# Moving three modulation chunks and one expert's gate load in a two-layer diffusion step on one core

## The reference, cut to what matters

```python
def ada_modulation(cond, w, b):
    m = jax.nn.silu(cond) @ w + b                 # 1024 -> 6 * 1024, for each layer and each of two conds
    ...
for l in range(DEPTH):                            # DEPTH = 2
    sh1, sc1, g1, sh2, sc2, g2 = ada_modulation(cond, ada_w[l], ada_b[l])
    h = modulate(x, norm_mix_g[l], sh1, sc1)
    m = attention(h) if l == 0 else multi_scale_pool(h)
    x = x + g1 * m
    h = modulate(x, norm_ffn_g[l], sh2, sc2)
    x = x + g2 * hierarchical_moe(h, ...)         # 4 groups x 8 experts, top 2 in the best group
```

## Time and profile before

| | us |
|---|---|
| three runs | 866.87, 872.73, 871.26 |
| median | 871.26 |
| profiled execution, its own time | 872.78 |
| its span | 870.7 |
| bytes moved by DMA in it | 294.42 MB |

### The profile page before, as it was taken

One profiled execution on the slowest core, in us unless ns is written; L12 is line 12 of the kernel. 1 busy time (PEld: TensorE's weight loads), 2 busy tenths in 40 slices (PEclk: granted clock), 3 DMA queues, 4 the chain that ended last, 5 costly groups with the idle time before them and its releaser, 6 DMA issues.

```text
span 870.7 us, 12882 instructions
## 1 busy us (share of the span) xinstructions
PE 731.4 (84%) x4560; PEld 405.2 (47%) x4560; DVE 352.0 (40%) x830; ACT 141.3 (16%) x342; POOL 175.7 (20%) x275
## 2 busy tenths in 40 slices
PE   4899989999976999999889763877899999797760
PEld 3333433467834655555445431735555545344430
DVE  2222548642245244444333332556244444333233
ACT  3111154531352000000000001544000000000000
POOL 0000400000002143333323120001133343332220
PEclk9999999999986899999999996787799999999995
DMA  9999849841864899999999953976699999999935
GB/s 345 428 435 422 234 151 415 315 194 47 362 269 164 323 418 419 419 416 420 417 418 422 420 238 130 419 325 205 214 421 416 421 415 423 419 422 419 414 131 217
DMA packets 41979, 294.42 MB, mean 338 GB/s; under 512 B 10872, under 2 KB 12336, under 8 KB 22864
## 3 DMA queue, kind: packets, MB, share of 16 engines
q1 hardware_dynamic: 29248, 275.51, 77.7%
q0 software_dynamic: 10880, 13.26, 5.0%
q10 hardware_dynamic: 1808, 5.06, 1.4%
HBM read 293.24 MB, written 22.02 MB: 362 GB/s over the span
## 4 chain that ended last, share of the span: by engine, by line
PE 64%; DMA 19%; SPq 6%; DVE 5%; issue 3%; ACT 1%; POOL 0%; POOLq 0%; DVEq 0%
PE bank L1578 21%; PE bank L1602 9%; DMA ring<-in_moe_w_in 8%; PE bank L1326 7%; PE bank L1251 4%; DMA ring<-in_moe_w_out 4%; PE bank L1425 3%; DMA ring<-in_ada_w 3%; PE bank L1556 3%; SPq L392 2%; DMA adaw<-results 2%; PE bank L1433 2%; PE bank L1468 2%; PE bank L1385 2%; DMA adaw<-in_ada_w 1%
## 5 line engine op out<-in xcount | busy, mean ns | idle before, releaser
L1578 PE MATMUL bank<-ring,qkv 128*64 128x256 f32 x1440 | 175.2, 397 | 23.2 <-issue 11.6
L1578 PEld LDWEIGHTS bank<-ring,qkv 128*64 128x64 f32 x1440 | 110.2, 143 | 74.5 <-issue 22.4
L547 POOL DMA_INDIRECT results<-adaw,scur x65 | 67.8, 1043 | 286.4 <-DVE adaw L1124 253.2
L1101 DVE COPY qkv<-bank 128x512 f32<-128x512 f32 x64 | 44.3, 692 | 194.5 <-PE bank L1556 174.3
L805 ACT ACTIVATE qkv<-bank 128x128 f32<-128x128 f32 x64 | 17.8, 278 | 445.7 <-PE bank L1578 411.1
L1602 PE MATMUL bank<-ring,qkv 128*64 128x512 f32 x360 | 87.1, 604 | 1.2 <-DVE qkv L1113 0.8
L537 POOL DMA_INDIRECT adaw<-rows,gcur x57 | 59.2, 1039 | 44.3 <-issue 28.0
L1326 PE MATMUL bank<-ring,hT 128*128 128x512 f32 x144 | 63.5, 596 | 1.3 <-DVE hT L879 1.3
L1113 DVE COPY qkv<-bank 128x128 f32<-128x128 f32 x64 | 18.7, 292 | 75.7 <-PE bank L1587 74.5
L1122 DVE SCALAR_TENSOR_TENSOR adaw<-qkv,wcur 128x512 f32<-128x512 f32 x64 | 48.1, 752 | 2.3
L1124 DVE SCALAR_TENSOR_TENSOR adaw<-bank,wcur,adaw 128x512 f32<-128x512 f32 x64 | 48.1, 751 | 2.3
(11 more groups left out here) (236 smaller groups left out, 839.7 us busy)
## 6 DMA issues: line engine op xcount, KB each, us to landing
ring<-in_moe_w_in SPq DMA_DIRECT2D x44, 2048.0 KB, 25.2
ring<-in_moe_w_out SPq DMA_DIRECT2D x45, 1024.0 KB, 33.3
adaw<-in_ada_w SPq DMA_DIRECT2D x16, 2048.0 KB, 11.2
adaw<-in_moe_w_in SPq DMA_DIRECT2D x10, 2048.0 KB
ring<-in_ada_w SPq DMA_DIRECT2D x8, 2048.0 KB, 12.1
xT<-in_moe_w_in SPq DMA_DIRECT2D x10, 1536.0 KB
hT<-in_moe_w_out SPq DMA_DIRECT2D x10, 1024.0 KB
ring<-in_attn_w_qkv SPq DMA_DIRECT2D x3, 2048.0 KB, 36.1
```

The lines of the kernel that those rows point to most:

```text
L547: pool.indirect_dma_start(res, bass.IndirectOffsetOnAxis(ap=scur[:, p, :], axis=0), yout[:, p], None, bounds_check=res_limit, oob_is_err=F ...
L1101: V.tensor_copy(xgT[:, p], bank[2][:, :]).then_inc(xgT_ready, 1)
L1578: last = T.matmul(bank[p][64 * a:64 * a + 64, 0:2 * P], xk[:, k % 4, k // 4], w[k // IN_X if b > RING else 0][:, k % IN_X if b > RING else ...
```

## The change

The diff does four things. (1) Chunks 21 to 23 are no longer loaded in the attention and the router stage of layer 0. Their places become the gate places of ring places 3, 0 and 1; SP issues them after the weights of the first extra tile, each after the last `gate_up` that reads its place. TensorE multiplies them after the extra tiles, before it signals `extras_over`; the copy, the spreading and the bias of this set follow there. (2) The vectors of the first 21 chunks are added on VectorE ahead of the router. (3) SP loads the fifth expert's gate weights (L381 before, L383 after) in the attention, where it has waited for chunk 19's product. (4) In both layers `rows_by_token(4)` and `(5)` come after the prefix sum on TensorE. GpSimd's clearing of `xg` waits for chunk 20 and no longer for 23.

```diff
@@ modulation chunks: places
-        ADA_AT = [TAIL, LEFT, RIGHT, HIGH0, HIGH1] + [(i + 2) % 3 for i in range(5, 2 * NCH - 2)] + [LEFT, LEFT]
+        TAIL, LEFT, RIGHT, HIGH0, HIGH1, RING3, RING0, RING1 = range(8)
+        ada_place += [ring[:, b, 0:KD * ACH] for b in (3, 0, 1)]
+        ADA_AT = [TAIL, LEFT, RIGHT, HIGH0, HIGH1] + [(i + 2) % 3 for i in range(5, 2 * NCH - 3)] + [RING3, RING0, RING1]
...
@@ SP
-            for i in range(8, 2 * NCH - 1):
+            for i in range(8, 2 * NCH - 3):
                 load_ada(i)
...
                 if l == 0:
+                    sp.wait_ge(ada_mm, 20)
                     load_out(l, 3, 3, s_wout[3])
                     sp.dma_start(ring[:, 3, KD * FE:2 * KD * FE], moe_w_in[l, 3, :, KD * FE:2 * KD * FE]).then_inc(s_win[3], 16)
+                    load_in(l, RING, RING, s_win[RING])
                     sp.wait_ge(pv_mm, NU // 4)
...
                     sp.wait_ge(ada_vec, 2)
-                    sp.wait_ge(ada_mm, 22)
...
-                load_in(l, RING, RING, s_win[RING])
-                if l == 0:
-                    load_ada(2 * NCH - 1)
...
-                    sp.wait_ge(ada_vec, 4)
+                    sp.wait_ge(ada_vec, 3)
...
                     load_extra(0)
+                if l == 0:
+                    for i, s in ((21, NE - 5), (22, NE - 2), (23, NE - 1)):
+                        sp.wait_ge(gu_mm, s + 1)
+                        load_ada(i)
@@ GpSimd
-                    pool.wait_ge(ada_mm, 24)
+                    pool.wait_ge(ada_mm, 21)
@@ ScalarE
-                if l == 0:
-                    set_copy(3)
                 for n in range(6):
                     keep(n)
...
                 extra_tiles(act, n_extra, extra)
+                if l == 0:
+                    set_copy(3)
@@ VectorE
-                if l == 0:
-                    dve.wait_ge(ada_vec, 4)
-                    modulation(2, 0, 5, 6)
-                    modulation(2, 1, 0, 6)
-                    V.memset(ss[:, 17:18], 0.0).then_inc(mods_ready, 1)
...
             norm_dve(0, 0, 4, 3, lambda k: hT[:, k, 0:CTX])
+            dve.wait_ge(ada_vec, 3)
+            modulation(2, 0, 5, 6)
+            vectors_of(2, 1, 0, 4 * KD + KD // 2)
+            V.memset(ss[:, 17:18], 0.0).then_inc(mods_ready, 1)
             router(0)
             experts(0)
...
             scales(1, 1, 8)
+            dve.wait_ge(ada_vec, 4)
+            vectors_of(3, 1, 4 * KD + KD // 2, 6 * KD)
             scales(1, 4, 24)
@@ TensorE
-                if l == 0:
-                    ada(21)
-                    ada(22)
...
-                rows_by_token(4)
-                rows_by_token(5)
-                if l == 0:
-                    ada(23)
-
                 pe.wait_ge(over_ready, l + 1)
...
                 last.then_inc(over_mm, 1)
+                rows_by_token(4)
+                rows_by_token(5)
...
-                if l == 0:
-                    vectors(3)
...
+                pe.wait_ge(mods_ready, 3 + l)
                 rows_T(0, 0, old=False)
...
                 extra_tiles(pe, n_extra, extra)
                 if l == 0:
+                    for i in range(SETS[3], 2 * NCH):
+                        ada(i)
                     T.matmul(bank[3][:, 0:2], ident, C("sel")[:, 0:2], start=True, stop=True).then_inc(extras_over, 1)
+                    vectors(3)
```

More of the change, by code:

```diff
@@ L198, in build @@
                      high[:, 0:KD * ACH], high[:, KD * ACH:KD * D]]
-        TAIL, LEFT, RIGHT, HIGH0, HIGH1 = range(5)
-        ADA_AT = [TAIL, LEFT, RIGHT, HIGH0, HIGH1] + [(i + 2) % 3 for i in range(5, 2 * NCH - 2)] + [LEFT, LEFT]
-        ADA_USE = [ADA_AT[:i + 1].count(ADA_AT[i]) for i in range(2 * NCH)]
+        TAIL, LEFT, RIGHT, HIGH0, HIGH1, RING3, RING0, RING1 = range(8)
+        ada_place += [ring[:, b, 0:KD * ACH] for b in (3, 0, 1)]
+        ADA_AT = [TAIL, LEFT, RIGHT, HIGH0, HIGH1] + [(i + 2) % 3 for i in range(5, 2 * NCH - 3)] + [RING3, RING0, RING1]
+        ADA_SIGNAL = [at if at < RING3 else at - RING3 for at in ADA_AT]
+        ADA_USE = [ADA_SIGNAL[:i + 1].count(ADA_SIGNAL[i]) for i in range(2 * NCH)]
         ADA_PRIOR = [max([j for j in range(i) if ADA_AT[j] == ADA_AT[i]], default=-1) for i in range(2 * NCH)]
@@ L238, in build @@
         SETS = (0, 4, 10, 21, 2 * NCH)
-        SET_BANK, VECTOR_BANK = (0, 1, 2, 0), (2, 0, 1, 1)
+        SET_BANK, VECTOR_BANK = (0, 1, 2, 0), (2, 0, 2, 2)
         def set_of(i):
@@ L373, in load_ada @@
                     sp.wait_ge(ada_mm, ADA_PRIOR[i] + 1)
-                sp.dma_start(ada_place[ADA_AT[i]], ada_w[i // NCH, i % NCH]).then_inc(s_adaw[ADA_AT[i]], 16)
+                sp.dma_start(ada_place[ADA_AT[i]], ada_w[i // NCH, i % NCH]).then_inc(s_adaw[ADA_SIGNAL[i]], 16)
             def load_in(l, e, b, arrived):
@@ L859, in modulation, with vectors_of @@
             def modulation(n, l, a, b):
-                cols = bank[VECTOR_BANK[n]][:, l * 2 * NMOD + 2 * a * KD:l * 2 * NMOD + 2 * b * KD]
-                m = mods[:, l, a * KD:b * KD, :]
+                vectors_of(n, l, a * KD, b * KD)
+            def vectors_of(n, l, a, b):
+                cols = bank[VECTOR_BANK[n]][:, l * 2 * NMOD + 2 * a:l * 2 * NMOD + 2 * b]
+                m = mods[:, l, a:b, :]
                 order(V.tensor_tensor(m, cols.rearrange("p (m c) -> p m c", c=2),
-                                      bias[:, l, a * KD:b * KD].unsqueeze(2).to_broadcast([P, (b - a) * KD, 2]), ALU.add))
+                                      bias[:, l, a:b].unsqueeze(2).to_broadcast([P, b - a, 2]), ALU.add))
             def scales(l, i, first):
@@ L1244, in ada @@
                     pe.wait_ge(cond_ready, 2)
-                pe.wait_ge(s_adaw[ADA_AT[i]], 16 * ADA_USE[i])
+                pe.wait_ge(s_adaw[ADA_SIGNAL[i]], 16 * ADA_USE[i])
                 out = bank[SET_BANK[n]]
@@ L1618, in _ @@
                 hidden_T(0, 0, old=False)
-                pe.wait_ge(mods_ready, 3 + l)
                 gate_rows()
```

## The result

| | before | changed |
|---|---|---|
| median of 20 runs each, us | 870.12 | 866.49 |
| lowest and highest | 866.87, 875.37 | 863.14, 871.51 |
| ratio, 95% interval | | 0.9949 [0.9931, 0.9967] |
| profiled execution, its own time | 872.78 | 863.50 |
| its span | 870.7 | 861.5 |

The change gains half a per cent, 2.9 to 6.0 us by the interval of the ratio (4.4 at its middle; the medians are 3.6 apart). The forecast of 864.3 has the sign, and the result lies in its range, but the gain in it was too large: 7.0, counted from the 871.26 of the three runs before, where twenty runs gave 870.12. From that base it would have been 863.1, 3.4 from the result in place of 2.2, so this much of its nearness is luck. The two profiled executions are 9.2 us apart. So there are two things to explain: why the 7.0 became 4.4, and why the profiles differ by more than the medians.

The account below looks back on a forecast made before the run. Layer 0's expert pass was taken as a DMA-bound stream whose end moves with its start, set by the router. Terms -8.7 + 0.5 + 1.2 = -7.0 gave 865.8 for the profiled execution, 864.3 for the median; range 859 to 869.

Parts of the forecast that it names:

- The bound: Layer 0's expert pass: a DMA stream of fixed length, bytes over rate, whose end moves by as much as its start.
- The rival by which the change doesn't do what it says: End of layer 0's pass not tied to its start; only losses remain: +1.7, 873 us; chance 0.05.
- Step (a): Layer 0's router, turned logits to L1039: without chunks 21 to 23 as short as layer 1's, 8.0 us gained.
- Step (b): Layer 0's router, L1040: no longer beside GpSimd's clearing of xg, 0.9 us gained, or nothing if the two are unlinked.
- Step (c): Layer 0's router, the tables (L1526): as fast as layer 1's, 1.3 us gained, lower end 0.
- The gather, 6.5 us: Layer 0, first gather's issue to first tile: 6.5 us, between ends 4.88 and 8.2; first tile 8.7 us sooner.
- The joint, 0.5 us: End of layer 0's pass: moved chunks' vectors delay the second sum of results by 0 to 1.4 us, 0.5 lost.
- The rival with late chunks: End of layer 0's pass: chunk 23 takes 33.28 us to land, net +2.5, 873.8 us; chance 0.12.
- Layer 1, 1.2 us lost: Layer 1's router: last transposes wait for the prefix sum, L1039 0.6 us later, 1.2 lost in all (0.6 to 1.6).

Follow-up runs that it names:

- e7: Changed kernel with the old order of the last transposes and layer 0's sixth-expert gate load held until the first tile is turned: 857.74 us, ratio 0.9877.
- e8: As e7, with the sixth expert's gate load held back in layer 1 too: 859.02 us, ratio 0.9872.
- e1: The changed kernel again, no edit: 867.23 us, ratio 0.9948 to the kernel before.
- e6: Changed kernel with GpSimd's clearing of the gather tiles held back until the prefix sum is made: 867.92 us, one run.
- e10: Changed kernel with layer 0's fifth-expert gate load put back behind the logits, chunks left at the joint: 868.06 us, ratio 0.9962.
- e9: Changed kernel with GpSimd's clearing started by the last of the transposes that VectorE too waits for: 867.55 us, one run.
- e2: Changed kernel with the last eight router transposes put back ahead of the prefix sum in both layers: 864.21 us, ratio 0.9918.
- e3: Changed kernel with layer 0's sixth-expert gate load held back until the first gathered tile is turned: 862.84 us, ratio 0.9895.

## Why the prediction was right, and where it was too high

**The bound.** Right. B was 228.4 to 229.0 us in all kernels but e7 and e8, while A went from 45 to 34.5: the stream has its own length and moves with its start. The rival by which the change doesn't do what it says is out.

**Step (a), 8.0 us.** A1 fell from 20.6 to 12.1 (mean of changed, e1, e6, e10): 8.5. Right: TensorE's product of the counts was mostly at half clock after its gap, as taken from layer 1 (2.57 to 2.77 us, but 1.67 in the changed kernel's first profile), and the new order cost 0.4 here in place of 0.6.

**Step (b), 0.9 us.** L1048 to the tables fell from 6.98 to 6.12 us, and e9 shows the cause. I had left open that the clearing might block VectorE in the attention instead, for up to 1.8 us. It does not lengthen it: from the end of chunk 10's product to the turned logits it is 126.8 and 126.3 us before, and 125.7 to 127.1 in the ten profiles with the change.

**Step (c), 1.3 us: failed.** The tables stayed at half clock, 2.79 us, in every profile with the new order, and ran in 1.57 in e2, which has the old one. In e7 and e8, with the old order too, they took 1.56 and 1.69. The 1.53 us of the earlier trace rows was layer 1's, and it does not carry over: in layer 1 the tables take 1.43 to 1.55 us in either order (1.68 once), directly behind 16 transposes of the residual without a gap (3.75 us in the changed kernel), while in layer 0 only eight stand there, and the last eight run after the tables. So with the new order layer 0 reaches its tables still at half clock. The runs show that the order decides it there; what in it does, beyond that, they do not. It is also why the price of the new order in layer 0, which I put at 0.6, was about 1.5 up to the gather's issue (22.95 against 21.43): 0.3 up to L1048 and 1.2 in the tables.

**The gather, 6.5 us: mis-sized.** It took 7.6, near the end that the earlier trace rows gave, and not the middle; alone it takes 3.3 (e3), below both of my ends. The 5.01 of the earlier trace rows was never the gather's time: TensorE was busy with the spreading of the last set until then. The 4.88 of the earlier trace rows had a load 3.5 us ahead of it. The rule of the Trainium skill (DMA: Bandwidth & Descriptors, on queues and rings) pointed to the short end, and the trace does not bear that out: a load of 5 us, issued 0.1 us behind the gather and not ahead of it as I had it, cost the gather 4.3. By which way the load holds it up, no run shows.

Together the first refill came 6.9 us sooner (44.9 to 38.0), where I had the first tile 8.7 sooner.

**The joint, 0.5 us.** Nothing in C (26.5 against 26.5, mean of changed, e1, e6, e10), and 0.4 if one leaves out the extra tile's `gate_up`, whose clock differs, and counts from the tile's last product (17.0 against 16.7). Chunk 23's landing came out to 0.1 us, and TensorE kept its full clock, so the lower part of 0 to 1.4 held. The rival with late chunks is out: 15.0 us after the last load, not 23.6.

**Layer 1, 1.2 us lost.** D rose from 33.7 (34.41 and 33.03) to 35.4: 1.7. Of this 0.4 is the product of the counts, which stands ahead of the moved transposes (2.35 us on the mean of the two profiles before, 2.77 after). Without it the new order cost 1.4 up to the tables, against 1.2: L1048 came 0.4 later, where I had 0.6, and the tables another 1.0. The step was right, by the mechanism that it gave.

Sum of what was measured: -6.9 + 0.4 (B) + 0 + 1.7 = -4.8 us, against 4.4 and 4.5 from the two ratios. The rest of the 9.2 between the first two profiled executions lies where the code is the same. 1.5 is in A: the product of the counts took 1.67 us and the first refill came 7.13 us after the tile, where e1 has 2.65 and 7.79. 1.4 is ahead of the turned logits, most of it chunk 10's product. 1.0 is in layer 1's mixer, whose last third had a granted clock of 0.86 after and 0.74 before, and 0.74 again in e1. 0.7 is in D, which lost 1.0 between these two. The small rest, 0.2 us, goes the other way. Mean granted clock was 0.926 and 0.934.

## What to carry to other kernels

When a long wait is taken away, read what else it held back. Here it kept a 2 MB load out of the way of a small transfer on the critical path, and one added wait (e3) was worth about as much as the change itself (4.4 us by the medians, 3.9 in A). Work that covers another engine's latency should not be moved behind the product that waits for it, even when it looks like it is in the way. And a price read from another stage holds for that stage's order of work: in layer 0 the tables took 1.57 or 2.79 us by which transposes stood ahead of them.

## What the runs showed of the hardware

- The first tile of a gather of 128 rows of 2 KB started 3.3 us after the gather's issue with no load in SP's queue (e3, e7, e8), 5.4 to 5.8 with a 2 MB load issued 3 us ahead of it (layer 1; 4.88 once, 6.72 once), and 7.5 to 7.7 with one issued 0.1 us behind it (layer 0). Here a load right behind the gather's issue was worse than one ahead of it.
- A VectorE scaling from SBUF to SBUF that meets a GpSimd clearing waits to its very end (1.64 us in e9 and 1.04 in the kernel before, in place of 0.18); an operation with an input in PSUM doesn't (L1039 in the kernel before, 0.19).
- One kernel's runs spread over 8 us on one core. Products of the same code took 1.92 or 3.48 us (granted clock 1.00 and 0.54), and 13.97 or 16.59 (1.00 and 0.84), by when the granted clock went back to 2.4 GHz. A profile is one draw of this: two profiles 9.2 us apart stood for kernels 4.5 us apart.
